# Gate columns in one product, expert queries in three single-pass products, and four waits and the last sums of the expert stage placed elsewhere

## The reference

```python
mq, mk, mv, mo, mg, gq, gk, gv, gr, glr = split(z)          # z = h @ w_in, h: tokens and context
gates = (mg + gate_b).reshape(bz, n, 2, 2, ML_HEADS)        # 16 columns: input and forget gates
alpha = einsum('bndr,drk->bndk', glr.reshape(bz, n, 2, GLA_RANK), lr_w2) + alpha_b   # 32 columns
...
q = (xb @ wq).reshape(PEER_BLOCK, PEER_HEADS, 2, PEER_QDIM // 2)     # expert queries, 1024 -> 2048
s = einsum('tphq,phkq->tphk', q, keys)                      # 128 keys for each of 16 halves
top_s, top_i = lax.top_k(s, PEER_TOPK)                      # then the best 16 of 16 x 16 pairs
...
act = gelu(einsum('tpkd,td->tpk', u_tab[idx], xb))
return einsum('tpk,tpkd->td', g * act, v_tab[idx])          # 16384 experts of width 1024
```

## Time and profile before

| | |
|---|---|
| three runs | 1717.67 us median, 1713.7 to 1718.57 |
| the profiled execution, its own time | 1720.85 us |
| its span | 1719.1 us (1.75 us lie around it) |
| TensorE busy | 1647.3 us, 96% |
| VectorE, ScalarE busy | 1063.3 us (62%), 666.3 us (39%) |
| mean granted TensorE clock | 0.983 |

### The profile page before, as it was taken

One profiled execution on the slowest core, in us unless ns is written; L12 is line 12 of the kernel. 1 busy time (PEld: TensorE's weight loads), 2 busy tenths in 40 slices (PEclk: granted clock), 3 DMA queues, 4 the chain that ended last, 5 costly groups with the idle time before them and its releaser, 6 DMA issues.

```text
span 1719.1 us, 27652 instructions
## 1 busy us (share of the span) xinstructions
PE 1647.3 (96%) x10246; PEld 1404.3 (82%) x10246; DVE 1063.3 (62%) x1920; ACT 666.3 (39%) x956; POOL 32.6 (2%) x80
## 2 busy tenths in 40 slices
PE   7999898999998999999999999999999999999996
PEld 6676476789997355678789999999899788888885
DVE  6992222356543326735239999898784677777775
ACT  4235112254432123221134465554445444444442
POOL 2002000000000000100000000000000000000000
PEclk9999899999999999999999999999999999999998
DMA  6353935435553122030417777755456677777773
GB/s 254 122 205 109 369 126 185 151 126 194 174 192 137 49 74 98 1 113 36 171 64 228 220 226 229 216 164 158 135 157 203 216 230 232 233 233 230 231 233 101
DMA packets 92284, 293.23 MB, mean 171 GB/s; under 512 B 10256, under 2 KB 43152, under 8 KB 77488
## 3 DMA queue, kind: packets, MB, share of 16 engines
q1 hardware_dynamic: 92160, 292.11, 52.7%
q10 hardware_dynamic: 48, 0.07, 0.0%
HBM read 274.31 MB, written 17.83 MB: 170 GB/s over the span
## 4 chain that ended last, share of the span: by engine, by line
PE 89%; DVE 6%; DMA 3%; ACT 1%; issue 0%; SPq 0%; DVEq 0%; ACTq 0%
PE ps L379 89%; DMA ring<-in_w_mod 1%; DVE big L1237 1%; DMA ring<-in_peer_u 1%; DVE split_ring L1715 1%; DVE big L1146 1%; DVE x L1850 0%; DVE big L1764 0%; DVE big L1768 0%; DVE big L1766 0%; ACT split_ring L2196 0%; DMA x<-in_x 0%; DMA kept_acts<-acts 0%; DVE big L1635 0%; DVE hh L1213 0%
## 5 line engine op out<-in xcount | busy, mean ns | idle before, releaser
L379 PE MATMUL ps<-split_hh,split_ring 128*128 128x256 f32 x3072 | 378.5, 284 | 4.9 <-DVE split_ring L1715 4.4
L379 PEld LDWEIGHTS ps<-split_hh,split_ring 128*128 128x128 f32 x3072 | 371.0, 192 | 6.4 <-issue 3.8
L379 PE MATMUL ps<-split_ring 128*128 128x512 f32 (+1 forms) x2048 | 363.9, 341 | 3.6 <-DVE split_ring L1715 2.3
L379 PEld LDWEIGHTS ps<-split_ring 128*128 128x128 f32 x2048 | 314.9, 189 | 52.6 <-DVE split_ring L1715 2.9
L1715 DVE TENSOR_TENSOR split_ring<-ring,split_ring 128x1024 fp32r<-128x1024 f32 x256 | 311.3, 1219 | 47.7 <-ACT split_ring L2196 45.6
L379 PE MATMUL ps<-hh,ring 128*128 128x256 f32 (+3 forms) x1104 | 278.3, 413 | 11.6 <-DVE hh L1444 7.2
L379 PEld LDWEIGHTS ps<-hh,ring 128*128 128x128 f32 (+2 forms) x1104 | 207.4, 189 | 81.0 <-issue 53.5
L2203 ACT ACTIVATE split_ring<-ring 128x1024 fp32r<-128x1024 f32 x128 | 135.9, 1062 | 188.3 <-DMA ring<-in_peer_v 188.3
L2196 ACT ACTIVATE split_ring<-ring 128x1024 fp32r<-128x1024 f32 x128 | 135.2, 1057 | 86.9 <-DMA ring<-in_peer_u 86.8
L379 PE MATMUL ps<-split_ffn_h,split_ffn_w 128*128 128x256 f32 x1056 | 130.3, 287 | 3.5 <-ACT split_ffn_h L2071 3.5
L379 PEld LDWEIGHTS ps<-split_ffn_h,split_ffn_w 128*128 128x128 f32 x1056 | 129.2, 194 | 4.6 <-issue 3.9
(11 more groups left out here) (291 smaller groups left out, 1475.0 us busy)
## 6 DMA issues: line engine op xcount, KB each, us to landing
ring<-in_peer_u SPq DMA_DIRECT2D x128, 512.0 KB, 4.0
ring<-in_peer_v SPq DMA_DIRECT2D x128, 512.0 KB, 3.7
ring<-in_w_mod SPq DMA_DIRECT2D x24, 1024.0 KB, 5.2
ring<-in_ffn_in SPq DMA_DIRECT2D x22, 1024.0 KB, 5.0
ring<-kept_acts SPq DMA_DIRECT2D x128, 128.0 KB, 3.4
ring<-in_ffn_out SPq DMA_DIRECT2D x11, 1024.0 KB, 4.9
ring<-in_w_out SPq DMA_DIRECT2D x8, 1024.0 KB, 10.4
ring<-in_peer_wq SPq DMA_DIRECT2D x8, 1024.0 KB, 5.0
```

The costliest lines, as they stand in the source:

```text
L379: return nc.tensor.matmul(out, lhsT, rhs, start=start, stop=stop, skip_group_check=True)
```

## The change

The columns of `ig`, `fg` and `glr` are laid out in one block of 128, and one product takes the place of three: input gates on rows 0 to 35, forget gates from row 64, the 32 rank columns at 36 to 51 and 100 to 115. ScalarE and VectorE read the same bank one after the other. `glr` and `lr_w` now have 128 partitions; the rows that are no rank columns have zero weights in `lr_w`, so that `alpha` stays the same.

The queries go by three `float32r` products per item as in the FFN, with the same three places for the split weights. `h_high` is made slice by slice, `h_low` before the last seven products instead of after them.

Four waits are placed anew: `high_u(0)` stands two copies earlier in ScalarE's order; `turn_keys(1)` and `keep_keys(1)` stand at `g = 1` and `g = 2` instead of 16; ScalarE makes the high parts of the first two weighted activations before the Gelu of the last chunk; SyncE loads the stored activations of chunks 4 and 5 before it waits for the last stores. The sums of the last chunk are reported one by one, and VectorE adds them in the order in which TensorE makes them. A Sqrt of one column is put ahead of ScalarE's last loop.

```diff
+LAST_SUMS = (2, 3, 4, 5, 6, 7, 0, 1)
...
-            both("ig", "act", w[:, :, 0:36], 36)
-            both("fg", "dve", w[:, :, 36:72], 36)
-            both("glr", "act", w[:, :, 72:104], 32)
+            both("gates", ("act", "dve"), weights("gates", 0, KD * P).rearrange("p (k c) -> p k c", k=KD))
...
             for i in range(PH):
-                project(("pq", i), ("act",), "peer_wq", i, h_peer)
+                bank = begin(("pq", i), "act")
+                weights("peer_wq", i)
+                high, low = (w[:, i % 3, :].rearrange("p (m k c) -> p m k c", m=2, k=KD) for w in (fw_high, fw_low))
+                pe.wait_ge(flag("query_weights_split"), i + 1)
+                for n, (w, rhs) in enumerate(((high, h_high), (low, h_high), (high, h_low))):
+                    if i == 0 and n == 2:
+                        pe.wait_ge(flag("h_split"), 1)
+                    for m in range(2):
+                        for k in range(KD):
+                            if i == 0 and n == 0 and m == 0:
+                                pe.wait_ge(flag("h_high_ready"), k + 1)
+                            last = mm(bank[:, m * T:(m + 1) * T], w[:, m, k, :], rhs[:, k, :],
+                                      n == 0 and m == 0 and k == 0, n == 2 and k == KD - 1)
+                last.then_inc(made, 1)
+                release()
...
-            pe.wait_ge(flag("x_final"), plan.bank["final_sum"] + 1)
-            for k in range(KD):
-                if k % 2 == 0:
-                    pe.wait_ge(flag("final_squares"), k // 2 + 1)
+            pe.wait_ge(flag("x_final"), LAST_SUMS.index(plan.bank["final_sum"]) + 1)
+            for n, k in enumerate(LAST_SUMS):
+                if n % 2 == 0:
+                    pe.wait_ge(flag("final_squares"), n // 2 + 1)
...
+            whole = flag("whole_weighted")
+            for q in range(2):
+                sp.wait_ge(flag(f"act_out{q}"), 16 * (NE // 4))
+                sp.wait_ge(whole, q + 1)
+                load_act(4 + q, q)
             for n in range(2):
                 sp.wait_ge(flag(f"act_out{n}"), 16 * (NE // 2))
-            whole = flag("whole_weighted")
-            for q in range(2):
-                sp.wait_ge(whole, q + 1)
-                load_act(4 + q, q)
...
+            def query_low(n):
+
+                s.wait("query_weights_high", n + 1)
+                v.tensor_tensor(fw_low[:, n % 3, :], ring[:, (queries_at + n) % RING, :], fw_high[:, n % 3, :].bitcast(F32),
+                                ALU.subtract).then_inc(flag("query_weights_split"), 1)
+
+            query_low(0)
+            query_low(1)
             for i in range(4):
                 bank = s.product(("mix2_out", i))
...
-            s.wait("h_high_ready")
+            s.wait("h_high_ready", KD)
+            v.tensor_tensor(h_low, h, h_high.bitcast(F32), ALU.subtract).then_inc(flag("h_split"), 1)
+            for n in range(2, PH):
+                query_low(n)
             dve.wait_ge(made, number(("pq", PH - 1)))
-            v.tensor_tensor(h_low, h, h_high.bitcast(F32), ALU.subtract).then_inc(flag("h_split"), 1)
...
+            def query_high(n):
+
+                at = queries_at + n
+                act.wait_ge(in_ring[at % RING], 16 * (at // RING + 1))
+                if n >= 3:
+                    act.wait_ge(made, number(("pq", n - 3)))
+                a_(fw_high[:, n % 3, :], ring[:, at % RING, :], ACT.Copy).then_inc(flag("query_weights_high"), 1)
+
+            query_high(0)
+            query_high(1)
             squares_by_pair("peer_sum", lambda i: s.after(("mix2_out", i), "dve"))
             std_of("peer_sum", D, T, 0)
-
-            s.wait("h_peer", KD)
-            a_(h_high, h[:, :, :], ACT.Copy).then_inc(flag("h_high_ready"), 1)
+            for k in range(KD):
+                s.wait("h_peer", k + 1)
+                a_(h_high[:, k, :], h[:, k, :], ACT.Copy).then_inc(flag("h_high_ready"), 1)
+            query_high(2)
...
             for i in range(PH):
                 copy_out(("pq", i), pq[:, 2 * i:2 * i + 2, :], halves)
+                if i + 3 < PH:
+                    query_high(i + 3)
```

More of the change, by code:

```diff
@@ L252, in program @@
         g_rows = area.take(6, 512)[0:36]
-        glr = area.take(512)[0:32]
-        lr_w = area.take(2, T)[0:32]
+        glr = area.take(512)
+        lr_w = area.take(2, T)
         reset = area.take(2, 512)
@@ L789, in _ @@
                 project(("mq", i), ("act",), "w2_mq", i, hk)
-            after("glr")
+            after("gates", "act")
             pe.wait_ge(flag("lr_loaded"), 16)
@@ L1493, in _ @@
             f_raw, f_log, f_sum, gd, run = (g_rows[:, i] for i in (1, 2, 5, 3, 4))
-            bank = s.product("fg")
-            s.took("fg", v.tensor_scalar(f_raw, bank[0:36, :], col("f_b", 0, 36), None, ALU.add))
-            s.after("fg")
+            bank = s.product("gates")
+            s.took("gates", v.tensor_scalar(f_raw, bank[64:100, :], cols("f_b")[64:100], None, ALU.add))
+            s.after("gates", "dve")
             v.tensor_scalar(f_log, f_raw, -CLIP, None, ALU.max).then_inc(flag("f_clipped"), 1)
@@ L1516, in _ @@
             link(running(f_sum, f_raw, bwd, lat_, True, add_, 0.0, None))
-            s.after("ig", "act")
+            s.after("gates", "act")
             i_gate = g_rows[:, 0]
@@ L2088, in _ @@
             std_of("lat_sum", D, T, 0)
-            bank = s.product("ig")
-            s.took("ig", a_(g_rows[:, 0], bank[0:36, :], ACT.Identity, bias=col("ig_b", 0, 36)))
-            copy_out("glr", glr, lambda b: b[0:32, :])
+            bank = s.product("gates")
+            a_(g_rows[:, 0], bank[0:36, :], ACT.Identity, bias=col("ig_b", 0, 36))
+            s.after("gates", "dve")
+            copy_out("gates", glr, lambda b: b)
             s.wait("f_clipped")
```

80 lines of the change are left out of this document (45 added, 35 removed).

## The result

The changed kernel takes 1689.57 us (median of four runs, 1686.99 to 1691.33), the kernel before on the same chip 1716.7 us (four runs): a ratio of 0.9847, 95% interval 0.9831 to 0.9862, or 27.1 us less. The forecast was 1688.7. The profiled execution took 1686.99 us with a span of 1685.3.

A forecast was written before the change was run, and what follows sets the result against it. TensorE, with 89% of the chain that ended last, was taken as the bound by its work and waits. Terms -13.85 - 6.4 - 1.65 - 4.1 - 1.5 - 1.5 = -29.0 from 1717.67 gave 1688.7 us, range 1682 to 1697.

The forecast's parts named there:

- Gates: Gate stage: one product of 128 rows replaces the `ig` and `glr` copies' two products; -13.85 us, at worst -13.0.
- The lag of VectorE's chain: Gate rows: VectorE's chain comes 13.0 us earlier, `mk` products 13.85; the 0.8 us lag is below VectorE's 4.55 us wait.
- Queries: Query products: seven split products save 8.0 us, the first loses 1.6; together -6.4, bounds -8.0 and -4.0.
- First chunk: First expert chunk: earlier high part of `u` lets TensorE start sooner; -1.65 us, bounds 0 and -2.0.
- Keys: One-hot rows at `g = 16`: moving the key transposes and copy removes TensorE's 4.08 us wait; -4.1, bounds -3.0 and -4.3.
- Start of the second half: Transition to second half: `v(4)` issued earlier, so chunk 4 starts 0.6 to 2.2 us sooner; -1.5 us taken.
- the other case: Start of the second half: if the store's landing no longer mattered, the gain would be 3.6 us.
- End: Last chunk: earlier adds, but `final_sum` in bank 1 waits for all 16; -1.5 us, between -0.9 and -3.8.
- Early Sqrt: End: removes a 1.28 us table load hidden in the wait for TensorE; price nothing, 1.28 were the wait gone.
- Rivals: Split products save nothing 0.10; mixer takes back gates 0.07; transition waits return 0.07; slow clock 0.02; loads not overlapping 0.01.
- the rival of the slow clock: Queries: short first matmuls keep TensorE at 1.2 GHz throughout; +34.5 against -22.6 gives 1729.6 us; chance 0.02.

The follow-up runs named there:

- loads and first `u` back: Changed kernel with loads of activations 4 and 5 behind the last stores' wait again, first high part of `u` behind all key copies; 1686.74 us (0.9843).

## Why the prediction was right

- Gates, -13.85: measured 13.85 and 13.86. The lag of VectorE's chain never came to matter.
- Queries, -6.4: the seven later products saved 8.02 as reckoned (40.32 us instead of 48.34), the first one lost 2.21 instead of 1.6, together -5.8. Its copies stand 5.76 apart, the first at 824.63 (825.1 said). Of the 2.21 us, 1.7 are the clock: it was at 0.50, its level of 1.2 GHz, from 814.8 to 821.5, behind a wait of 4.07 us; the kernel before, which waited 3.62 us, had it for half as long (from 829.4 to 832.8). The Trainium skill's rule that a weight load overlaps a matmul only with other row groups ("TensorE: Matmul & The Clock Gate", Part 3) does not hold in these rows: 48 pairs in 5.76 us are 0.12 us each. (That Part also names a background weight buffer as a target for such loads; no row shows whether it is what serves here.)
- First chunk, -1.65: -1.79, and 1.78 when it was undone. The bound of -2.0 was too near: where the clock falls after the wait of 2.98 us, the step is worth some 3.3 (1.78 and 1.5 in the first 28 chunks).
- Keys, -4.1, bound -4.3: the term was mis-sized. Undoing it cost 5.3 by the column and 5.9 between chunks 76 and 100. The prediction took the wait alone; the 1.7 us of work lost at the lower clock behind it are in the trace of the kernel before too. D to E shrank by 6.73 us in all: 6.0 are this step, and 0.8 lie between chunks 28 and 76, where no code differs.
- Start of the second half, -1.5: the step that failed. "`v(4)` can be issued between 1337.5 and 1339.2" is 5.7 to 7.4 us after the last Gelu, and so it was (6.0 to 7.2 in seven kernels). But it was reckoned from an issue at 8.0 us that belonged to the one execution of the earlier trace rows, whose three loads took 2.84 us; the two other traces with the old order have 6.9 and 6.6. E to F is 13.2 to 14.2 us in the seven (mean 13.7) and 13.9 and 13.6 in those two, so the runs give no gain. What the prediction named as the other case (the store's landing no longer matters, 3.6) gives 0.9 alone, and 2.2 with VectorE's order changed.
- End, -1.5: -2.1 to -2.3 in six of the eight traces with this order; in the two others `final_sum` ran for 6.5 us instead of 5.3, at 0.56 of the clock instead of 0.69, and it was -0.9 to -1.0. Both lie in the bounds. That bank 1 must wait for all 16 adds was right and was the costly part: 3.5 us more could be had there.
- Early Sqrt, nothing: right. The Trainium skill's 2.66 us for a switch ("ScalarE: Activation LUTs", "What ACT_TABLE_LOAD costs") are not in the rows: the load takes 1.28 us, no drain stands on either side of it, and here it is hidden.
- Rivals: none of the five came. TensorE was back at the full clock in the first query product, and there was no wait of several microseconds in the mixer, none at `g = 16`, and chunk 4 waited 1.60 us, as said. In the rival of the slow clock, eight slow products would cost 34.4 us, not 34.5, and it takes five of them, not four, to use up 22.6; its chance of 0.02 hardly hangs on it.

The steps' own values add to -13.85 - 5.8 - 1.8 - 6.0 - 0 - (0.9 to 2.3) = -28.4 to -29.8 us; the two comparisons of medians gave -27.1 and -28.5. The largest terms were right by their mechanism. That the sum of -29.0 came out so near is luck in part: keys, too small by 1.9, stood against the second half's start, too large by 1.5, and the queries, too large by 0.6.

## What to carry to other kernels

A wait of TensorE of 2 us or more should be priced with the granted clock of the windows behind it, not by its length alone; here that added 1.7 us to 4.1. Before a wait of one profiled execution is priced, look whether another execution has it: 1.3 us of the start of the second half stood in one trace only. Judge a step of a few microseconds by the stretch of the timeline that it touches, and look for columns of unchanged code, which show what the medians scatter by.

## What the runs showed of the hardware

- The same instructions on TensorE ran at two paces under a granted clock of 1.00: 0.3533 and 0.3467 us per pair of a 512-column and a 256-column product, for stretches of hundreds of products. Over 124 chunks of 8 pairs that is 6.6 us, of the size of the 10 us over which one kernel's runs spread; that it makes them is not shown, since only one execution of each has a trace. In the trace of "loads and first `u` back" the pace changed once at a stop of TensorE of 0.06 us, and more often at none; what decides between the two was not found. Two long and two short products in turn give 0.3483 mostly, eight and eight 0.3492.
- A wait of 2.98 us was followed by a clock of 1.00 in two executions and of 0.62 in another; waits of 4.1 and 4.2 us by 0.57 and 0.62. Before chunk 4 waits of 2.06, 2.24, 2.28 and 2.34 us were followed by 0.50 for more than 3 us, and waits of 1.08 to 2.01 us, in six executions, by 1.00. `final_sum`, after a wait of 4.03 us, had 0.69 and took 5.33 us, and 0.56 and 6.48 us in another execution.
- The last store of the activations landed in 3.97 to 4.23 us in three executions with its loads behind it, and in 4.14 to 5.31 us in seven with two loads of the same size beside it.
- A change of ScalarE's table took 1.28 us, with 0.02 us between it and the copy before it and as much before the Sqrt behind it.
